# Where TensorE's operands begin in SBUF: weights and x tiles on multiples of 512 bytes, feed-forward product tiles 64 bytes further apart

## What is computed

```python
def swiglu(h, w_gate, w_up, w_down):
    return (jax.nn.silu(h @ w_gate) * (h @ w_up)) @ w_down

for i in range(DEPTH):
    x = x + 0.5 * swiglu(rmsnorm(x, ffn1_norm[i]), ffn1_w_gate[i], ffn1_w_up[i], ffn1_w_down[i])
    h = rmsnorm(x, mix_norm[i]) @ w_in[i]
    ...                                  # attention, convolution, long convolution
    x = x + y @ w_out[i]
    x = x + 0.5 * swiglu(rmsnorm(x, ffn2_norm[i]), ffn2_w_gate[i], ffn2_w_up[i], ffn2_w_down[i])
```

## Time and profile before

| | us |
|---|---|
| median of 3 runs | 3362.08 |
| the runs | 3359.32 to 3362.18 |
| span of the profiled execution | 3360.4 |
| TensorE matmul busy | 3228.2 (96%) |
| VectorE busy | 1812.3 (54%) |
| GpSimd busy | 1835.2 (55%) |
| ScalarE busy | 748.6 (22%) |

### The profile page before, as it was taken

One profiled execution on the slowest core, in us unless ns is written; L12 is line 12 of the kernel. 1 busy time (PEld: TensorE's weight loads), 2 busy tenths in 40 slices (PEclk: granted clock), 3 DMA queues, 4 the chain that ended last, 5 costly groups with the idle time before them and its releaser, 6 DMA issues.

```text
span 3360.4 us, 44069 instructions
## 1 busy us (share of the span) xinstructions
PE 3228.2 (96%) x14534; PEld 2578.4 (77%) x14534; DVE 1812.3 (54%) x1971; ACT 748.6 (22%) x1260; POOL 1835.2 (55%) x1026
## 2 busy tenths in 40 slices
PE   8999998899999999999889999999999999999998
PEld 6788875578888778876567888788777877888886
DVE  7661277663313765138754331586768886753312
ACT  2110126422201111014532220111122322222200
POOL 5556651066666656663036666644455455666665
PEclk9999999999999999999999999999999999999999
DMA  4222320022323322331012222322122222223322
GB/s 155 81 86 96 113 76 26 9 86 94 100 94 103 110 79 89 100 107 56 13 44 88 98 96 98 118 76 69 63 85 69 76 69 70 94 94 94 97 96 81
DMA packets 77430, 281.26 MB, mean 84 GB/s; under 512 B 9382, under 2 KB 9766, under 8 KB 76776
## 3 DMA queue, kind: packets, MB, share of 16 engines
q1 hardware_dynamic: 74016, 268.58, 24.5%
q10 hardware_dynamic: 3272, 10.79, 0.9%
HBM read 277.24 MB, written 2.10 MB: 83 GB/s over the span
## 4 chain that ended last, share of the span: by engine, by line
PE 79%; DVE 15%; issue 4%; ACT 2%; DVEq 0%; DMA 0%; ACTq 0%; SPq 0%
PE bank L505 24%; PE bank L510 23%; PE bank L509 23%; DVE short L1938 1%; PE bank L640 1%; PE bank L725 1%; PE bank L790 1%; DVE square_sum L1727 1%; DVE xbc L2276 1%; DVE y L1970 1%; DVE x_lo L1717 1%; DVE scaled L2114 1%; PE bank L799 1%; DVE att_qk L2212 0%; DVE reach L2369 0%
## 5 line engine op out<-in xcount | busy, mean ns | idle before, releaser
L451 POOL TENSOR_SCALAR w_hi<-raw 128x1024 fp32r<-128x1024 f32 x504 | 554.8, 1101 | 1451.4 <-PE bank L505 1443.0
L454 POOL TENSOR_TENSOR w_lo<-raw,w_hi 128x1024 fp32r<-128x1024 f32 x504 | 1267.5, 2515 | 42.0
L505 PE MATMUL bank<-x_hi,w_hi 128*128 128x512 f32 x2896 | 1151.3, 398 | 47.7 <-DVE x_lo L1717 21.6
L510 PE MATMUL bank<-x_hi,w_lo 128*128 128x512 f32 x2896 | 1134.6, 392 | 0.0
L509 PE MATMUL bank<-x_lo,w_hi 128*128 128x512 f32 x2896 | 1134.0, 392 | 0.0
L505 PEld LDWEIGHTS bank<-x_hi,w_hi 128*128 128x128 f32 x2896 | 547.8, 189 | 183.4 <-issue 66.4
L510 PEld LDWEIGHTS bank<-x_hi,w_lo 128*128 128x128 f32 x2896 | 547.6, 189 | 116.2
L509 PEld LDWEIGHTS bank<-x_lo,w_hi 128*128 128x128 f32 x2896 | 547.8, 189 | 114.5 <-issue 4.1
L505 PE MATMUL bank<-hidden_hi,w_hi 128*128 (+1 forms) x880 | 342.3, 389 | 0.0
L509 PE MATMUL bank<-hidden_lo,w_hi 128*128 (+1 forms) x880 | 342.3, 389 | 0.0
L510 PE MATMUL bank<-hidden_hi,w_lo 128*128 (+1 forms) x880 | 342.3, 389 | 0.0
(11 more groups left out here) (382 smaller groups left out, 3229.1 us busy)
## 6 DMA issues: line engine op xcount, KB each, us to landing
raw<-in_w SPq DMA_DIRECT2D x504, 512.0 KB, 3.6
dft<-in_dft ACTq DMA_DIRECT2D x2, 1536.0 KB, 6.6
out<-x SPq DMA_DIRECT2D x4, 512.0 KB, 2.6
mask<-in_mask ACTq DMA_DIRECT2D x1, 1536.0 KB, 7.2
x<-in_x SPq DMA_DIRECT2D x2, 512.0 KB, 5.9
x<-in_x SPq DMA_DIRECT2D x1, 1024.0 KB, 8.8
filt_cos<-in_dft_filter ACTq DMA_DIRECT2D x2, 512.0 KB, 6.5
filt_sin<-in_dft_filter ACTq DMA_DIRECT2D x2, 512.0 KB, 8.1
```

The costliest lines, as they stand in the source:

```text
L451: nc.gpsimd.tensor_scalar(w_hi[:, s % 2, :], raw[:, s, :], 1.0, 0.0, ALU.mult, ALU.add).then_inc(w_rounded, 1)
L454: nc.gpsimd.tensor_tensor(w_lo[:, s % 2, :], raw[:, s, :], w_hi[:, s % 2, :].bitcast(F32), ALU.subtract).then_inc(w_split, 1)
L505: first = nc.tensor.matmul(out, hi_w, hi, start=start, stop=False)
L510: return nc.tensor.matmul(out, lo_w, hi, start=False, stop=stop)
```

## The change

Seven edits, all of them in where tensors lie or how large they are, with two lines of code that follow from a smaller `b_time`:

```diff
+STEP = 16
...
         raw = sb("raw", [P, RAW, BLOCK * P])
+        sb("weights_apart", [P, 96])
         w_hi = sb("w_hi", [P, 2, BLOCK * P], F32R)
...
-        hidden_hi = sb("hidden_hi", [P, FC, T], F32R, ffn_mem)
+        hidden_steps = sb("hidden_hi", [P, FC, T + STEP], F32R, ffn_mem)
+        hidden_hi = hidden_steps[:, :, 0:T]
         hidden_lo = sb("hidden_lo", [P, FC, T], F32R, ffn_mem)
...
-        decay_late = sb("decay_late", [P, TT // 2, CW], F32, ffn_mem)
         ffn_mem.close()
 
         filt_mem = ExitStack()
-        sb("kept_hi", [P, KEPT * T], F32, filt_mem)
+        sb("kept_hi", [P, KEPT * (T + STEP)], F32, filt_mem)
...
-        sb("kept_lo", [P, KEPT * T], F32, filt_mem)
+        sb("kept_lo", [P, (FC - KEPT) * STEP + KEPT * T], F32, filt_mem)
...
         taps_sum = sb("taps_sum", [P, CW], F32, filt_mem)
+        decay_late = sb("decay_late", [P, TT // 2, CW], F32, filt_mem)
...
-        b_time = sb("b_time", [P, CH, P], F32, left_mem)
+        b_time = sb("b_time", [P, CH - 1, P], F32, left_mem)
...
-                for ch in range(CH):
+                for ch in range(CH - 1):
                     last = nc.tensor.transpose(bank[2][:, ch * P:(ch + 1) * P],
...
-                    nc.scalar.activation(b_time[:].rearrange("p c n -> p (c n)"), bank[2][:], ACT.Copy
+                    nc.scalar.activation(b_time[:].rearrange("p c n -> p (c n)"), bank[2][:, 0:(CH - 1) * P], ACT.Copy
```

## The result

The changed kernel takes 3374.32 us (median of seven runs, 3369.47 to 3376.11) against 3362.08 for the kernel before (seven runs, 3359.32 to 3364.37). The ratio is 1.0035, with a 95% interval of 1.0024 to 1.0046: slower by 12.2 us. The forecast was no change, 3361.7, with a range of 3333 to 3374. Two executions further down, one of g1 (10360.27 us) and one of g4 (3419.7 us, at a mean granted clock of 0.923 where the others have 0.987), stand far above the others of their kernels and are left out of the medians given.

What follows compares the result with a forecast made beforehand. TensorE's 12000 float32r matmuls at 0.2267 us, 81% of the span, were taken as the bound. Layout terms counted 0 and transposes 0.4 us, so 3360.4 became 3360.0; with 1.7 for the runs' median, 3361.7, range 3333 to 3374.

Steps and rivals of the forecast that it cites:

- The bound: TensorE: 12000 float32r matmuls of `product`, 0.2267 us from start to start, set the time: 2720 us, 81% of the span.
- Weights and x moved together: Weights and x tiles go from 128 to 0 past a multiple of 512: 0 us, bounds 128 less to 40 more.
- the nothing for `decay_late`: `decay_late` moves into memory of the last hidden tiles; no instruction or wait changes with it: 0 us.
- the 0.4 us for the transposes: One transpose less in each of four groups on TensorE, 0.11 us each: 0.44 us saved.
- The other engines: VectorE, ScalarE and GpSimd were to keep their speed at the new addresses, a slower GpSimd split staying hidden: nothing.
- Hidden tiles: Hidden tiles 2112 bytes apart, 2640 matmuls on them: 0 us, bounds 28 us less and 9 us more.
- the four steps of 0.230: Steps in `spread` with stream and load both at 320, 0.0033 us above the dense runs; not taken for the address.
- the two mixed steps: Steps at `spread` with 192 bytes between stream and load, 0.23 us each, read as no nearer 0.216 than dense runs.
- The upper bound: Largest loss per float32r matmul taken from `spread`, 0.0033 us: 9 us on hidden tiles, 40 us on all 12000.
- The slower rival: Hidden streams at odd multiples of 64 cost more lines or meet the weight load: 9 us, 3370.4; chance 0.17.
- The faster rival: New places end 0.0107 us of operand interference or line crossing per matmul: 28 us on hidden tiles, 128 on all; chance 0.28.
- The rule: Only the port pair VectorE and GpSimd share makes engines wait; by it the whole layout is worth 0 us.

Runs made afterwards that it cites:

- g1: Changed kernel with hidden_lo brought back to 0 from the weights, the 64-byte steps of hidden_hi kept: 3374.96 us, ratio 1.0038.
- g4: Changed kernel without the steps, hidden_hi alone 128 bytes from the weights, hidden_lo and x at 0: 3366.86 us, ratio 1.0013.
- e1: Changed kernel without the 64-byte steps, so that every operand lies at a multiple of 512: 3361.69 us, ratio 1.0001.
- g2: Changed kernel without steps and weight shift, sel_hi, ident_hi, after_hi and a_rows of `spread` moved to the weights' place: 3359.78 us, ratio 0.9994.
- f3: Changed kernel without steps, w_hi at 128, w_lo at 256, streamed tiles at 384, so only w_lo is away: 3400.43 us, ratio 1.0115.
- f1: Changed kernel without steps, both weight tensors at 256 and every operand that `product` streams at 384: 3412.96 us, ratio 1.0153.
- e4: Changed kernel without steps and weight shift, hidden_hi and hidden_lo both 384 bytes from the weights: 3377.08 us, ratio 1.0042.
- e3: Changed kernel without steps and weight shift, hidden_lo alone 384 bytes from the weights: 3366.87 us, ratio 1.0014.
- f4: Changed kernel without the weight shift, hidden_hi in 16-byte steps in place of 64, hidden_lo at 0 from the weights: 3375.47 us, ratio 1.0039.
- e2: Changed kernel without the weight shift: weights and x back at 128, hidden tiles against them as in the changed kernel: 3374.67 us, ratio 1.0036.
- g3: Changed kernel without steps, w_hi at 256, w_lo and streamed tiles at 384, so only w_hi is away: 3420.66 us, ratio 1.0172.

## Why the prediction was wrong

**The bound** was read rightly: TensorE's float32r matmuls, one behind another at 0.2267 us. The change moved that distance on 2640 of them, and the time followed one for one.

**Weights and x moved together: 0.** Right, shown by e1. Its ratio of 1.0001 (0.9991 to 1.001) also bears out the nothing for `decay_late`; the 0.4 us for the transposes is less than that interval can show.

**The other engines.** Right: VectorE, ScalarE and GpSimd keep their busy times. The copy behind the three transposes is shorter, as forecast, and hidden. The tile `b_time` in the changed kernel (min/median/max ns):

```profile
L1629 ACT ACTIVATE b_time<-bank x4: 491/492/492, 2491.3 to 2797.5; 128x384 f32<-128x384 f32 x4
```

**Hidden tiles: the step that failed.** It was "I take 0 us; the bounds are 2640 x 0.0107 = 28 us less and 2640 x 0.0033 = 9 us more". Measured is 0.0047 more, 12.4 us. The zero rested on two readings of the earlier trace rows. The first was "I don't take that for the address: `spread` stands behind semaphore waits and alternates two kinds of product", on the four steps of 0.230. g2 shows that they were the address: moved to the weights' place, with the same alternation and no wait inside either time, they fall to 0.2267. (Waits can do the same, as the settling in e1 shows; here it was not a wait.) The second was that "the two mixed steps" beside them, at 0.227 and 0.23, show a distance of 192 to be free. The cost falls on the matmuls that follow as well (f3, g1), so the step in which the displacement happens for the first time is not where it must show: that one took 226 ns, and three of the four behind it took 229 to 233, although stream and weights were 0 apart in them. One transition in a trace is no evidence for a dense run in that state.

**The upper bound** was too low for the same reason: 0.0033 was a mean over steps of which some had already recovered. Runs at a displaced place that repeats have 0.2326 (f1) and 0.2333 (e4) in the mean. The slower rival was therefore the right case, given 0.17, and undersized: 9 us where 12.2 came. Of its two mechanisms, "meets the weight load" agrees with a cost that hangs on the distance; "begin at odd multiples of 64" doesn't, since 384 and 16-byte steps cost as well (e3, f4). The measured 3374.3 lies 0.3 us past the range, whose top of 3374 was worked out from those four steps and a little more; that it comes so near is luck.

**The faster rival** fell. Its observation, that nothing in the rows could see the address because everything sat at 128, was right; but the common place was the best one, not a bad one. f4's scan has no distance under 0.2267, so the 0.0107 us over plain float32 do not hang on these places; what they are stays open.

**The rule.** The Trainium skill (SBUF — State Buffer, section "SBUF: two separate sides") has it that TensorE, ScalarE and VectorE's dedicated pair never wait on anyone. For engines waiting on each other the two windows of the earlier trace rows agree. Within TensorE the runs differ from the use that the prediction made of it: moving only the weights 128 bytes off the streamed tiles costs 50 us (f1), where the prediction read the page as 0 for the whole layout. The measurement decides.

**What is shown and what is not.** Shown: the cost hangs on the distance between streamed operand and weights. 0 and 256 let the steps settle at 0.2267; all others tried (16k apart from 256, 64k, 128, 384) don't. Absolute place (0 or 128: e1, e2), hi against lo (e4) and the address instruction (e3, e4, f4) don't matter. Argued and not shown: that it is two reads inside SBUF that meet. Open: why tile 8 of g1 has to settle again and tile 16 of f4 doesn't, and why g3 is dearer than f1. Distances under 16 bytes or not a multiple of 16, and other shapes and types, were not tried. No variant beats the kernel before.

## What to carry to other kernels

Where float32r matmuls over 512 columns stand one behind another, let the streamed tiles and the weights begin a multiple of 256 bytes apart, hi and lo weights and all streamed tiles alike; padding rows by 64 or 16 bytes to "spread" them loses 2%, 4.7 ns in 227, on those matmuls. Check such a layout by the distance between starts in the same dense 30 to 100 us of both traces: 131 matmuls where 134 stood name the operand, which a whole time 0.35% longer doesn't. And when one operand sits at the same place everywhere, the trace cannot price another: take the only odd rows in it as the best evidence there is, and widen the range to more than their mean.

## What the runs showed of the hardware

- A float32r matmul of 128x128 by 512 columns at a granted clock of 1.00 has a distance of 0.2267 us to the next, once settled, when stream and weights begin 0 or 256 bytes apart. At other distances the means of displaced matmuls are 0.228 (g4, the last matmul) to 0.235 (g3, the last matmul). The Trainium skill (TensorE: Matmul & The Clock Gate, section "Back-to-back issue gap") gives 512 / 2.4 + 2.5 = 215.8 ns as the gap of a single matmul; no twelve dense float32r matmuls in a row of any run here came under 0.2266 us.
- The settling takes up to ten matmuls after a wait, with steps of 0.224 to 0.240 us on the way in all but four cases (e1, all 62 stretches), and with displaced weights it never comes (f1, f3, g3: 0 of 62). A tile whose operands are all back at distance 0 can have to settle again: nine matmuls of 0.231, then 0.2267 (g1, tile 8).
- The effect is not local to the displaced load: loads of `w_lo` alone displaced lengthen two matmuls of three (396 and 397 against 389 ns, f3), and displacing `w_hi` alone (g3, 58.1 us) is dearer than displacing both (f1, 49.9 us).
- Slower matmuls give a part back where TensorE waits for others: in f1 the steps of over 0.3 us add up to 11.4 us less than in e1.
